# Spreading the decay and key factors by fp32r products of a 32-row block-diagonal tile

## The reference

```python
# gated DeltaNet: cumulative log-decay within a chunk, and its differences
gc = jnp.cumsum(chunks(g), axis=-1)
diff = gc[..., :, None] - gc[..., None, :]
decay = jnp.where(lower, jnp.exp(jnp.where(lower, diff, 0.0)), 0.0)
# block attention: RMS norm of each key vector per head, then scores with ALiBi
kh = rms_norm(k.reshape(bsz, seq, H, Dh), k_gain)
s_own = jnp.einsum("nqd,nkd->nqk", q_blk, k_own) * scale - slopes[:, None, None] * dist_own
```

## Time and profile before

| | |
|---|---|
| three timed runs | 1003.11 us (1002.99 to 1003.37) |
| the profiled execution | 1002.87 us, its span 1001.1 us |
| TensorE products busy | 994.9 us, 99% of the span |
| VectorE, ScalarE, GpSimd busy | 688.7, 440.0, 505.1 us |
| TensorE's granted clock | 1.00 of full speed throughout |

### The profile page before, as it was taken

How to read it: one execution, slowest core, us unless ns; L and a number is a source line. 1 busy time by engine, 2 the same in 40 slices (tenths; PEclk the granted TensorE clock), 3 DMA queues, 4 the chain that set the end, 5 groups by cost and what they waited for, 6 DMA issues and landing times.

```text
span 1001.1 us, 16467 instructions
## 1 busy us (share of the span) xinstructions
PE 994.9 (99%) x6826; PEld 876.2 (88%) x6826; DVE 688.7 (69%) x1084; ACT 440.0 (44%) x645; POOL 505.1 (50%) x289
## 2 busy tenths in 40 slices
PE   9999999999999999999999999999999999999998
PEld 7888999999999988788878788888899999999997
DVE  5896986766666486863547883687688776667745
ACT  7542543344433462444356664534244244443341
POOL 0364866667566433543252201635576675756741
PEclk9999999999999999999999999999999999999999
DMA  8332223331233212321221001223302332123312
GB/s 331 127 127 84 85 84 127 127 126 51 82 121 127 99 71 85 122 89 43 85 69 61 2 3 43 95 89 112 126 32 96 127 127 104 65 85 127 127 43 84
DMA packets 15770, 95.32 MB, mean 95 GB/s; under 512 B 2000, under 2 KB 2128, under 8 KB 5456
## 3 DMA queue, kind: packets, MB, share of 16 engines
q1 hardware_dynamic: 15696, 94.27, 26.4%
HBM read 92.16 MB, written 2.10 MB: 94 GB/s over the span
## 4 chain that ended last, share of the span: by engine, by line
PE 92%; DVE 3%; DMA 1%; ACT 1%; POOL 1%; SPq 0%; issue 0%; DVEq 0%; POOLq 0%
PE bank L1916 50%; PE bank L2044 32%; DMA raw<-stream 1%; POOL wlo L485 1%; PE bank L2336 1%; PE bank L2340 1%; PE bank L2450 1%; PE bank L2384 1%; PE bank L2362 1%; PE bank L2422 0%; PE bank L2439 0%; ACT sqx L606 0%; PE bank L2406 0%; PE bank L2396 0%; ACT whi L581 0%
## 5 line engine op out<-in xcount | busy, mean ns | idle before, releaser
L485 POOL TENSOR_TENSOR wlo<-raw,whi 128x1024 fp32r<-128x1024 f32 (+1 forms) x44 | 148.3, 3387 | 215.2 <-ACT whi L581 198.4
L2044 PE MATMUL bank<-t_ffn_hi,wlo 128*128 128x256 f32 x896 | 253.6, 283 | 0.0
L2044 PE MATMUL bank<-t_ffn_lo,whi 128*128 128x256 f32 x896 | 253.6, 283 | 0.0
L2044 PE MATMUL bank<-t_ffn_hi,whi 128*128 128x256 f32 x896 | 253.5, 283 | 0.0
L502 POOL TENSOR_TENSOR wlo<-sums,whi 128x512 fp32r<-128x512 f32 x128 | 170.4, 1354 | 120.3 <-ACT whi L695 120.1
L502 POOL TENSOR_TENSOR wlo<-raw,whi 128x512 fp32r<-128x512 f32 x96 | 158.7, 1667 | 39.3 <-ACT whi L695 39.3
L2044 PEld LDWEIGHTS bank<-t_ffn_lo,whi 128*128 128x128 f32 x896 | 172.0, 192 | 0.6
L2044 PEld LDWEIGHTS bank<-t_ffn_hi,whi 128*128 128x128 f32 x896 | 172.0, 192 | 0.6
L1916 PE MATMUL bank<-ahi,whi 128*128 128x512 f32 x432 | 171.2, 396 | 1.0 <-POOL wlo L485 1.0
L2044 PEld LDWEIGHTS bank<-t_ffn_hi,wlo 128*128 128x128 f32 x896 | 172.0, 192 | 0.0
L1916 PE MATMUL bank<-ahi,wlo 128*128 128x512 f32 x432 | 168.4, 390 | 0.0
(11 more groups left out here) (312 smaller groups left out, 1408.2 us busy)
## 6 DMA issues: line engine op xcount, KB each, us to landing
raw<-fast_in SPq DMA_DIRECT2D x32, 1024.0 KB, 4.9
raw<-stream SPq DMA_DIRECT2D x30, 1024.0 KB, 4.9
raw_down<-fast_in SPq DMA_DIRECT2D x18, 1024.0 KB, 7.0
raw<-stream SPq DMA_DIRECT2D x6, 512.0 KB, 6.3
x<-x_in SPq DMA_DIRECT2D x4, 512.0 KB, 6.9
out<-x SPq DMA_DIRECT2D x8, 256.0 KB, 2.0
raw<-stream SPq DMA_DIRECT2D x4, 256.0 KB, 6.1
memx<-mem_in SPq DMA_DIRECT2D x2, 512.0 KB, 10.6
```

Source lines behind the costliest of these rows:

```text
L485: ins = nc.gpsimd.tensor_tensor(wlo[:, u % RING, c0:c1], raw[:, u % RAW, c0:c1], whi[:, u % RING, c0:c1].bitcast(F32), ALU.subtract)
L2044: ins = E.matmul(psum[bank][:, HALF * h:HALF * (h + 1)], a, b[:, k, :], start=start and k == 0 and m == 0, stop=k == K2 - 1 and m == 2, sk ...
```

## The change

- The constants get 16 more columns: four 0/1 patterns over 32 rows.
- `gate_sums` stays. VectorE now casts the cumulative sums to an fp32r high part and makes the low part (`column_parts(0)`), TensorE turns the 32 columns into 32 rows (`decay_turn`, one fp32 transpose), and VectorE multiplies these rows with a 0/1 pattern into a tile of 32 rows and 4 x 128 columns in which each head has its own rows (`decay_blocks`). `prep_decay(c)` is then one fp32r product of 32 rows and 512 columns; the left operand picks the block's rows and is the same for all partitions.
- The key factors go the same way: `column_parts(1)` in `qk_norm_end`, `mk_turn`, `mk_blocks`, and `mk_spread(t)` as one product of 32 rows and 512 columns for each pair of heads. Its left operand is `pairs_pick`, 32 x 4 x 64, made by a cast in `qk_norm`.
- The lists of TensorE, VectorE and ScalarE change order around these steps. The semaphore signal `w_used` moves from `prep_decay(2)` to `prep(2)`.

```diff
+            def column_parts(i, src, values):
+                hi, lo = columns_of[i][:, 0, :], columns_of[i][:, 1, :]
+                link(V.tensor_copy(hi, src))
+                return V.tensor_tensor(lo, values, hi.bitcast(F32), ALU.subtract)
+            def spread_blocks(i, turned_rows):
+                rows = turned_rows.rearrange("p (s t) -> p s t", s=2).unsqueeze(1).broadcast_to([32, H, 2, DH])
+                own = cst[0:32, C_BLK + 4 * i:C_BLK + 4 * i + 4].unsqueeze(2).unsqueeze(3).broadcast_to([32, H, 2, DH])
+                return V.tensor_tensor(blocks[i].rearrange("p (h s) t -> p h s t", s=2), rows, own, ALU.mult)
...
             link(V.tensor_copy(gates[:, G_GC:G_GC + 2, :], psum[6][:, 64:96].rearrange("p (n m) -> p n m", n=2)))
+            V.tensor_copy(picks[:], cst[:, C_PICK:C_PICK + 4])
+            column_parts(0, psum[6][:, 64:80], psum[6][:, 64:80])
             V.tensor_tensor(gate(G_GT), gate(G_GL), gate(G_GC), ALU.subtract).then_inc(g_dve, 1)
             evacuate(17, cq[:, 1, :])
+            decay_blocks()
...
             def qk_norm():
                 dve.wait_ge(sqa_used, 3)
+                V.tensor_copy(pairs_pick[:], cst[0:32, C_PICK + 4:C_PICK + 8].unsqueeze(2).broadcast_to([32, 4, DH]))
                 mean(6, psum[7][:].rearrange("p (c j t) -> p j c t", c=NC_, j=4)[:, :, :, 0:2],
...
+                rk = ratt[:, 2:4, :, :].rearrange("p t c e -> p (t c e)")
+                column_parts(1, rk, rk)
                 for h in range(H):
...
+            def turn_columns(i, out, done):
+                E.transpose(out, columns_of[i][:].bitcast(F32).rearrange("p n m -> p (n m)"), ident).then_inc(done, 1)
+            def mk_turn():
+                pe.wait_ge(ratt_ready, 2)
+                pe.wait_ge(p_evac, 23)
+                turn_columns(1, psum[0][0:32, 0:P], mkbc_ps)
             def prep_decay(c):
                 if c == 0:
-                    pe.wait_ge(gates_ready, 1)
+                    pe.wait_ge(g_dve, 5)
...
-                for h in range(H):
-                    i = E.matmul(heads(PREP_BANKS[c][0])[:, h, :], gcol(G_G, h, c).broadcast_to([P, P]), upper,
-                                 start=True, stop=True)
+                i = E.matmul(psum[PREP_BANKS[c][0]][:], picks[0:32, c:c + 1].broadcast_to([32, P]),
+                             blocks[0], start=True, stop=True)
...
             def mk_spread(t):
-                for c in range(NC_):
-                    i = spread_pair(0, c * P, ratt[:, 2 + t, c, :])
-                i.then_inc(mkbc_ps, 1)
+                pe.wait_ge(mk_ready, t + 1)
+                E.matmul(psum[0][:], pairs_pick[:, 2 * t:2 * t + 2, :].rearrange("p e n -> p (e n)"),
+                         blocks[1], start=True, stop=True).then_inc(mkbc_ps, 1)
```

The order of the lists, with what moves:

```diff
 TensorE      in_part(18, 8, 0, 0, K2)
+             decay_turn()
              in_part(18, 8, 0, K2, KD)
...
              level_first(0, 4)
-             mk_spread(0)
+             mk_turn()
              mem_out(2)
              in_part(25, 11, 1, 0, 2)
+             mk_spread(0)
              in_part(25, 11, 1, 2, 4)
              mem_turn(3)
-             in_part(25, 11, 1, 4, 6)
              level_second(0, 4)
              mem_out(3)
              mem_scores(5)
+             mk_spread(1)
              level_first(0, 5)
-             in_part(25, 11, 1, 6, 8)
+             in_part(25, 11, 1, 4, 6)
              mem_turn(4)
              mem_scores(6)
              level_second(0, 5)
              mem_out(4)
-             mk_spread(1)
-             mem_scores(7)
+             in_part(25, 11, 1, 6, 8)
+             prep_decay(2)
              level_first(0, 6)
+             mem_scores(7)
              mem_turn(5)
-             prep_decay(2)
              prep_decay(3)
...
 ScalarE      level_copy(0, 6)
+             prep_decay(2)
              mem_weights(7, 0)
              mem_weights(7, 1)
              mem_copy(5)
-             prep_decay(2)
              prep_decay(3)
```

More of the change, by code:

```diff
@@ L58 @@
 C_SEL = C_REL + T
-C_N = C_SEL + 2
+C_BLK = C_SEL + 2
+C_PICK = C_BLK + 8
+C_N = C_PICK + 8
 S_G1, S_GM, S_G2, S_GMEM = 0, KD, 2 * KD, 3 * KD
@@ L116, in build @@
         gates, _, _ = place("gates", [P, 16, 16])
+        picks, _, _ = place("picks", [P, 4], F32R)
+        columns_of = [place(f"columns{i}", [P, 2, 16], F32R)[0] for i in range(2)]
         rowmax, _, _ = place("rowmax", [P, 4])
@@ L148, in build @@
         sqa, _, _ = place("sqa", [P, 4, T], at=z_at)
+        blocks_, _, _ = place("blocks", [32, 2 * H, P], F32R, at=xt_at)
+        blocks = (blocks_[:, :, DH:P], blocks_[:, :, 0:DH])
+        pairs_pick = place("pairs_pick", [32, 4, DH], F32R, at=z_at + 3 * T * 4)[0]
         one = T * 4
@@ L1529, in _, with decay_blocks, mk_blocks @@
             mean(4, turned_sums, token_sums(msq_[:, 16:32]), 1.0)
+            def column_parts(i, src, values):
[6 more added lines that the diff above has]
+                return V.tensor_tensor(blocks[i].rearrange("p (h s) t -> p h s t", s=2), rows, own, ALU.mult)
+            def decay_blocks():
+                dve.wait_ge(g_pe, 2)
+                spread_blocks(0, psum[6][0:32, P:2 * P]).then_inc(g_dve, 1)
+            def mk_blocks():
+                dve.wait_ge(mkbc_ps, 1)
+                spread_blocks(1, psum[0][0:32, 0:P]).then_inc(mk_ready, 1)
             mv_evacuate(0)
@@ L1592, in mk_scale @@
             def mk_scale(t):
-                dve.wait_ge(mkbc_ps, t + 1)
+                dve.wait_ge(mkbc_ps, t + 2)
                 V.scalar_tensor_tensor(out=mk[:, t, :], in0=psum[0][:], scalar=gain_qk[:, 0:1],
@@ L1768, in _ @@
             evacuate(24, z[:, 2, :])
-            mk_scale(0)
+            mk_blocks()
             mem_scale(3, 0)
@@ L1773, in _ @@
             mem_max(4, 1)
+            mk_scale(0)
             level_update(0, 4)
@@ L1777, in _ @@
             mem_max(5, 1)
+            mk_scale(1)
             mem_scale(4, 0)
@@ L1781, in _ @@
             mem_max(6, 1)
-            evacuate(25, z[:, 3, :])
+            mem_scale(5, 0)
+            mem_scale(5, 1)
             level_update(0, 5)
             mem_out(4)
-            mem_scale(5, 0)
-            mem_scale(5, 1)
             mem_scale(6, 0)
-            mk_scale(1)
+            evacuate(25, z[:, 3, :])
+            prep_decay(2)
             mem_max(7, 0)
@@ L1947, in spread @@
                 return E.matmul(psum[bank][:, c0:c0 + P], column, ident, start=True, stop=True)
[L1949 to L1956, removed]
             def x_spread(stage):
@@ L2262, in prep_decay @@
                 elif c == 2:
-                    pe.wait_ge(mk_ready, 2)
+                    pe.wait_ge(mk_ready, 3)
                 else:
                     pe.wait_ge(p_evac, 26)
-                for h in range(H):
-                    i = E.matmul(heads(PREP_BANKS[c][0])[:, h, :], gcol(G_G, h, c).broadcast_to([P, P]), upper,
-                                 start=True, stop=True)
-                    if c == 2 and h == 0:
-                        i.then_inc(w_used, 1)
+                i = E.matmul(psum[PREP_BANKS[c][0]][:], picks[0:32, c:c + 1].broadcast_to([32, P]),
+                             blocks[0], start=True, stop=True)
                 i.then_inc(prep_ps[0], 1)
@@ L2286, in prep @@
                     i = E.matmul(heads(kb)[:, h, :], qkv[:, 4 + h, cs], qkv[:, 4 + h, cs], start=True, stop=True)
+                    if c == 2 and h == 0:
+                        i.then_inc(w_used, 1)
                 i.then_inc(prep_ps[1], 1)
@@ L2542, in _ @@
             gate_sums()
-            in_tile(18, 8, 0)
+            in_part(18, 8, 0, 0, K2)
+            decay_turn()
+            in_part(18, 8, 0, K2, KD)
             att_stats(1)
@@ L2607, in _ @@
             mem_out(4)
-            mk_spread(1)
+            in_part(25, 11, 1, 6, 8)
+            prep_decay(2)
+            level_first(0, 6)
             mem_scores(7)
-            level_first(0, 6)
             mem_turn(5)
-            prep_decay(2)
             prep_decay(3)
@@ L2756, in constants @@
     c[:, C_SEL + 1] = i >= DH
+    r = (i % 16)[:, None]
+    n = np.arange(4)[None, :]
+    c[:, C_BLK:C_BLK + 4] = r // NC_ == n
+    c[:, C_BLK + 4:C_BLK + 8] = r % 8 // 2 == n
+    c[:, C_PICK:C_PICK + 4] = r % NC_ == n
+    c[:, C_PICK + 4:C_PICK + 8] = (r // 8 == n // 2) & (r % 2 == n % 2)
     return c
```

8 lines of the change are left out of this document (3 added, 5 removed).

## The result

The changed kernel takes 1007.2 us (median of six runs, 1006.38 to 1009.3) where the kernel before took 1003.04 in the same session (1002.81 to 1003.37). The ratio is 1.0046, 95% interval 1.0036 to 1.0056: slower by 0.46%. The forecast was 1006.0, slower, by a hole of 3.45 us before `mem_turn(0)`. The direction and the hole are as forecast; the time lies 0.3 us beyond the end of the range. The six runs show where that comes from: with the mean granted clock that each run's record gives, they are 1006.38, 1006.53 and 1006.53 at 1.000, 1007.88 at 0.998, and 1009.17 and 1009.3 at 0.997. The profiled execution is the one of 1009.3, with a span of 1007.5.

What follows compares the result with a forecast made beforehand. TensorE was taken as the bound (92% of the chain). Span 1001.1 + 3.45 (hole) - 0.4 (gain) = 1004.15, with 1.77 around it and 0.24 to the median 1006.2, stated as 1006.0; 8-in-10 range 1002.2 to 1006.9.

Steps and rivals of the forecast that it cites:

- The cast (the step that decides): `pairs_pick` in `qk_norm`: GpSimd's subtraction holds the cast for 4.23 us, leaving a 3.45 us hole on TensorE before `mem_turn(0)`.
- Nothing gives it back: After the hole before `mem_turn(0)`: every later instruction of the stretch waits on TensorE, so the 3.45 us stay lost.
- Rival A: At `pairs_pick`: the cast is not held and lasts 0.35 us, so 1002.7 us, down to 1001.3; chance 0.2.
- What follows from the hole: Work behind the hole before `mem_turn(0)`: only the hole's length, 3.45 us, was counted, with no term for TensorE's clock.
- The price of the short products: On TensorE: 0.60 us per spread between whole-array products, 0.35 for the others; 0.45 and 0.35 for the two transposes.
- The gain from there to 565 us: TensorE's saving brings `level_first(0, 6)` 1.07 us earlier, of which 0.4 us reaches 565 us.
- The step with ScalarE: Behind `level_first(0, 6)`: `prep_decay(2)` puts two exponentials, 1.03 us, ahead of the softmaxes, so `mem_copy(5)` ends where it did.
- a move into idle time: On VectorE: the second `mk_scale` leaves the full stretch after 540 us for the one before, where VectorE has idle time.
- After 565 us: VectorE's list is the old one from `pt` on, so the 0.4 us gain was carried on with no further loss.
- B: Cast not held and short products cost only 0.22 us each: more than 2 us faster, 1001.0 us; chance 0.04.
- C: The hole plus a second one: GpSimd's mask near 528 us holds the `ratt` scalings 1.27 us; 1007.3 us, chance 0.08.
- Near 466 us: Small VectorE operations for the gates end just before GpSimd's split at 471.25; slipping behind it would cost under 0.5 us.

Runs made afterwards that it cites:

- experiment 6: The changed kernel plus twelve unused TensorE products before `mem_turn(0)` and ScalarE's `prep_decay(2)` behind `mem_copy(5)`, cast left in place: 1005.64 us.
- experiments 2, e2_cast: The kernel before plus one cast of the same shape at the head of `qk_norm`, its result never read: 1008.03 us.
- experiment 3: The changed kernel with GpSimd's subtraction for weight tile 11 moved behind `masks(0, 2)`, cast left in place: 1004.25 us.
- experiment 9: `e6_key_later` with the decay products of chunks 2 and 3 back in their old fp32 form: 1002.54 us.
- e1_late: The changed kernel with the `pairs_pick` cast moved out of `qk_norm` to just before `qk_norm_end`: 1003.49 us.
- experiment 5: `e1_late` with ScalarE's `prep_decay(2)` put back behind `mem_copy(5)`, as in the kernel before: 1002.61 us.
- experiment 7: The kernel of experiment 5 with VectorE's `mk_scale(1)` moved behind `mem_scale(4, 1)`: 1002.02 us.
- experiment 10: Seven one-column VectorE memsets of an unused tile, added to the kernel before (1003.05 us) and to `e6_key_later` (1001.79 us).
- e6_key_later: The kernel of experiment 7: experiment 5's kernel with VectorE's `mk_scale(1)` behind `mem_scale(4, 1)`, 1002.02 us.
- e11_best_seven: `e6_key_later` with seven one-column VectorE memsets of an unused tile behind `evacuate(22)`: 1001.79 us.
- e3_fill: The changed kernel with twelve unused 512-column TensorE products added ahead of `mem_turn(0)`: 1006.51 us.
- e8_split_later: The kernel of experiment 3: the changed kernel with GpSimd's subtraction moved behind `masks(0, 2)`, 1004.25 us.

## Why the prediction was nearly right, and where it failed

**The cast (the step that decides): right.** Forecast 4.23 us and a hole of 3.45; measured 3.96 and 3.24. The 0.2 us of difference is the end of the cast: I let its own 0.35 us follow GpSimd's end, and it was over 0.13 behind it. "Nothing gives it back" was nearly right: 0.2 us come back by 551 us, and 3.03 remain (experiment 6). Rival A's doubt, that a repeated source over 32 partitions might run otherwise, is settled by experiments 2 and 3. The section "Who interferes with whom" of the Trainium skill's page "SBUF — State Buffer" (the later one blocks wholly) describes both the cast and the scalings of experiment 3.

**What follows from the hole: missed. This is the step that failed.** I priced the hole at its length alone and put nothing for the work behind it. In the trace, after 2.85 us without a product TensorE's granted clock fell to 0.50, and four steps took 7.33 us where 4.73 were due: 2.6 us. In the three runs in which the mean clock stayed at 1.000 the time is 1006.4 to 1006.5, inside my range; at a mean clock of 0.997 it is 1009.2 to 1009.3, and the median, 1007.2, lies between the two kinds. Against 1006.5 that is +2.8 us in two runs, +1.4 in one, none in three. Only one of them has a trace. In the others the clock may have fallen at the thin stretch near 552 us instead, which the prediction did not price either.

**The price of the short products: right for the spreads, too high for the transposes.** I had 0.60 for a spread between whole-array products and 0.35 for the others. Measured are 0.62 and 0.64, and 0.43 (experiment 9). For the transposes I had 0.45 and 0.35, and they are 0.11 and 0.14. By 502 us the gain was therefore 0.63 and not 0.38: -0.89 + 0.62 + 0.11 - 0.89 + 0.43 = -0.62.

**The gain from there to 565 us: too high.** Forecast total 0.4; measured 0.14 at 551 in the changed kernel, and none (+0.02) in `e1_late`. The step with ScalarE was right: its two exponential pairs ahead of the softmaxes take 1.0 us (experiment 5), and between the end of `level_first(0, 6)` and `pt` I had 0.67 us of the gain lost (1.07 to 0.4), where `e1_late` loses 0.59. The error lies ahead of it. I had the level end 1.07 us early, and less the shift it ends 0.57 early (543.84 in `e1_late`, 544.39 before). Of the missing 0.5 us, 0.3 are VectorE's `mk_scale(1)`, which I counted as a move into idle time and which stood on the path of `mem_turn(4)` (experiment 7: there the level ends 0.87 early). For the other 0.2 no run shows the cause. TensorE's saving in the stretch is worth about half (experiment 9).

**After 565 us: not foreseen.** I had VectorE's list as unchanged, and 0.34 us were lost at 586, from a cause that stays open (experiment 10).

Sum for a run at full clock: 1003.04 - 0.63 + 3.24 + 0.49 + 0.34 = 1006.48, where 1006.38 to 1006.53 was measured. In other terms: 3.03 us that remain of the hole, and 0.37 for the rest of the change (`e1_late`), give 1006.44. I had 3.45 for the hole and a gain of 0.4 for the rest. That 1006.0 came as near as it did is in part luck, for the hole was put 0.4 us too long and the rest 0.8 us too good.

**Rivals.** A and B did not happen. C did not either: the scalings of `ratt` ran at 533.20 in 0.37 us, and GpSimd's mask began at 533.65, behind them. Near 466 us, as forecast, no small operation met the split: the last gates operation began at 471.25 and took 0.18 us, and the split began at 471.63.

**Two kernels are better than both.** `e6_key_later` and `e11_best_seven` take 1002.02 and 1001.79 us, 1.2 and 1.3 us below the kernel before; both intervals end below 1 (at 0.9997 and 0.9996). 5.46 us of TensorE's fp32 work replaced brings about that much, once the cast meets no GpSimd work and ScalarE and VectorE keep their softmaxes first.

## What to carry to other kernels

Before an SBUF-to-SBUF cast, copy or scaling is added to VectorE, look up what GpSimd does at that moment, and give the cast the length to GpSimd's end, however small it is; to move either engine's work by one step can be all that is needed, if the other side is then looked up again. A hole on TensorE must be priced together with the work behind it at the lower clock, and as a spread between runs, not as a number. And work taken from the bounding engine is worth its length only where no other engine's chain takes over at once.

## What the hardware showed that was not expected

- The clock's fall is not the same in every run of the same kernel (1006.4, 1007.9 and 1009.2 us in the changed kernel, at mean clocks of 1.000, 0.998 and 0.997). The mean, given to three figures, does not tell everything: a run of `e2_cast` with 1.000 took 1007.6 us.
- It did not need a hole. In `e3_fill` it fell behind two windows in which TensorE was busy 1.85 and 1.49 of 2 us, while in the changed kernel's trace it stayed at 1.00 behind two such windows. Single runs of `e1_late` (1006.53 us at 0.997) and `e8_split_later` (1006.2 at 0.997) have the low mean without the hole before `mem_turn(0)`.
- In `e2_cast` the hole had nearly the same length (2.86 us), yet the clock was still 1.00 in the window from 511 to 513 us, where the changed kernel's was 0.50, and was back at 1.00 by 517.
- With seven instructions more that do nothing, an operation 75 us behind them started 0.35 us earlier, in one trace each (`e6_key_later`, `e11_best_seven`).
